# First block of a SwiGLU with block products: two k tiles by gate, then up columns, and token-sum chunks asked for by need

## What is computed

```python
x = x + jnp.concatenate([o_a, o_b], axis=-1) @ w_out[layer]
h = rms_norm(x, ffn_norm_w[layer])
gate, up = jnp.split(h @ w_gate_up[layer], 2, axis=-1)
x = x + (jax.nn.silu(gate) * up) @ w_down[layer]
```

## Time and profile before

| | |
|---|---|
| median of 3 runs | 1125.2 us (1123.52 to 1126.71) |
| the profiled execution | 1124.23 us |
| its span, first to last instruction | 1122.4 us |
| mean granted TensorE clock | 0.999 of full |
| busy PE, DVE, ACT, POOL | 1112.1, 900.1, 645.5, 53.0 us |
| instructions on PE | 5256 matmuls |
| transfers of w_gate_up and w_down | 176 and 88 of 512 KB |

### The profile page before, as it was taken

One profiled execution on the slowest core, in us unless ns is written; L12 is line 12 of the kernel. 1 busy time (PEld: TensorE's weight loads), 2 busy tenths in 40 slices (PEclk: granted clock), 3 DMA queues, 4 the chain that ended last, 5 costly groups with the idle time before them and its releaser, 6 DMA issues.

```text
span 1122.4 us, 15499 instructions
## 1 busy us (share of the span) xinstructions
PE 1112.1 (99%) x5256; PEld 936.2 (83%) x5256; DVE 900.1 (80%) x1222; ACT 645.5 (58%) x914; POOL 53.0 (5%) x138
## 2 busy tenths in 40 slices
PE   8999999999999999999999999999999999999998
PEld 7988888888888888888888888888888888888887
DVE  5578786587876667678988988988988889999887
ACT  7566776668654456454554554554554555655553
POOL 3000000000000000000000000000000020000000
PEclk9999999999999999999999999999999999999999
DMA  8666555545555455777787777777677786666665
GB/s 265 194 196 189 159 157 158 164 141 170 197 176 170 153 186 170 208 212 238 217 233 241 217 232 240 217 235 237 218 234 239 234 294 211 202 224 195 199 206 169
DMA packets 107558, 230.03 MB, mean 205 GB/s; under 512 B 8265, under 2 KB 19314, under 8 KB 107250
## 3 DMA queue, kind: packets, MB, share of 16 engines
q1 hardware_dynamic: 101346, 209.30, 60.3%
q0 software_dynamic: 5856, 19.93, 5.7%
q10 hardware_dynamic: 304, 0.14, 0.0%
HBM read 218.85 MB, written 10.49 MB: 204 GB/s over the span
## 4 chain that ended last, share of the span: by engine, by line
PE 93%; DVE 3%; DMA 2%; issue 1%; ACT 0%; SPq 0%; DVEq 0%; ACTq 0%
PE side L1928 22%; PE main L1700 22%; PE side L1930 11%; PE main L1703 11%; PE side L1898 4%; PE side L1899 4%; PE side L1900 4%; PE main L1899 3%; PE main L1900 3%; PE main L1898 3%; DMA raw<-in_w_down 1%; PE side L1824 1%; DMA raw<-in_w_in 1%; PE side L1723 1%; DVE w_lo L1542 1%
## 5 line engine op out<-in xcount | busy, mean ns | idle before, releaser
L985 ACT CAST w_hi<-raw 128x1024 fp32r<-128x1024 f32 x245 | 239.7, 984 | 162.2 <-PE side L1928 62.3
L1542 DVE TENSOR_TENSOR w_lo<-raw,w_hi 128x1024 fp32r<-128x1024 f32 x245 | 274.3, 1132 | 18.3 <-ACT w_hi L985 18.1
L1094 DVE TENSOR_TENSOR w_lo<-raw,w_hi 128x1024 fp32r<-128x1024 f32 (+3 forms) x156 | 178.6, 1154 | 108.1 <-ACT w_hi L765 105.8
L765 ACT CAST w_hi<-raw 128x1024 fp32r<-128x1024 f32 (+3 forms) x156 | 153.7, 994 | 142.3 <-PE main L1700 137.5
L1700 PE MATMUL main<-w_hi,hT_hi 128*128 128x512 f32 (+2 forms) x448 | 173.4, 388 | 1.7 <-DVE hT_lo L1115 1.2
L1703 PE MATMUL main<-w_hi,hT_lo 128*128 128x512 f32 (+2 forms) x448 | 169.1, 378 | 0.0
L1928 PE MATMUL side<-w_hi,hT_hi 128*128 128x512 f32 x400 | 155.6, 389 | 0.0
L1930 PE MATMUL side<-w_hi,hT_lo 128*128 128x512 f32 x400 | 155.6, 389 | 0.0
L1700 PE MATMUL main<-w_lo,hT_hi 128*128 128x512 f32 (+2 forms) x448 | 114.8, 378 | 0.0
L1928 PE MATMUL side<-w_lo,hT_hi 128*128 128x512 f32 x400 | 106.9, 389 | 0.0
L1700 PEld LDWEIGHTS main<-w_hi,hT_hi 128*128 128x128 f32 x448 | 84.8, 189 | 15.3 <-DVE hT_lo L1115 2.3
(11 more groups left out here) (283 smaller groups left out, 1853.0 us busy)
## 6 DMA issues: line engine op xcount, KB each, us to landing
raw<-in_w_gate_up SPq DMA_DIRECT2D x176, 512.0 KB, 4.8
raw<-in_w_down SPq DMA_DIRECT2D x88, 512.0 KB, 4.5
raw<-in_w_in SPq DMA_DIRECT2D x64, 512.0 KB, 3.8
raw<-in_w_out SPq DMA_DIRECT2D x32, 512.0 KB, 3.7
raw<-in_w_in SPq DMA_DIRECT2D x15, 384.0 KB, 5.1
squares<-hiddenT POOLq DMA_DIRECT2D x11, 512.0 KB, 5.1
hiddenT<-squares POOLq DMA_DIRECT2D x44, 128.0 KB, 5.4
raw<-in_w_ukv SPq DMA_DIRECT2D x8, 512.0 KB, 4.0
```

What stands on the lines that cost most here:

```text
L765: copy(w_hi[:, slot, 0:n], raw[:, slot, 0:n]).then_inc(s_hi, 1)
L985: copy(w_hi[:, n % RING, 0:cols], src).then_inc(s_hi, 1)
L1094: tt(w_lo[:, slot, 0:n], raw[:, slot, 0:n], w_hi[:, slot, 0:n].bitcast(F32), ALU.subtract)\
L1542: tt(w_lo[:, n % RING, 0:cols], src, w_hi[:, n % RING, 0:cols].bitcast(F32), ALU.subtract)\
```

## The change

Block 0 gets the layout of the others: the same 14 items, loads and conversions, with the banks swapped (`first_banks`: `main` as plain banks, `side` as m banks), the mix, the adds and the gated product of the loop. Its first two items, k tiles 4 and 5, run together: 12 matmuls on the gate columns of both, then 12 on the up columns, so that the second half of `main` is wanted later. `sum_ff_tokens` moves to G0-2, the copy of its hi part on ACT to G0-1, `split_ff_sums` to item 0 of block 0; the adds of `out2` 3 move ahead of item 3's conversion on DVE. PE's wait for all `side` uses moves from the head of the loop to block 0's first paired item. Chunk c of the token sums is asked for at W1 + 0, 7, 16, 28 or 40 granules.

```diff
-W1 = B1 + FF_W * (NFF - 1)
+W1 = G0 + FF_W * NFF
+FIRST_TOGETHER = 2
-FF_SUMS_AT = 6
+FF_SUMS_AT = G0 - 2
+SUMS_FROM = (0, 7, 16, 28, 40)
...
+        banks = ([[side[0], side[1]], [side[2], side[3]]], (main[PG][0], main[PG][1], main[PU][0], main[PU][1]))
+        first_banks = ([[main[PG][t], main[PU][t]] for t in range(NT)], (side[0], side[1], side[2], side[3]))
...
-                pool.wait_ge(s_used, W1 + 2 * c)
+                pool.wait_ge(s_used, W1 + SUMS_FROM[c])
...
+            for m in range(len(FF_ITEMS)):
+                convert_item(0, m)
+                for s in steps_at(G0 + m):
+                    step(s)
+                if m == FF_AT["corner"]:
+                    take_corner(0, first_banks[1][0])
+                if m == FF_AT["multiply"]:
+                    act.wait_ge(s_inv, len(RMS))
+                    silu(0)
...
+            for m in range(len(FF_ITEMS)):
+                steps = steps_at(G0 + m)
+                for s in steps:
+                    if s[0] == "out2":
+                        step(s)
+                convert_item(0, m)
+                for s in steps:
+                    if s[0] != "out2":
+                        step(s)
+                if m == 0:
+                    split_ff_sums()
+                if 0 <= m - FF_AT["mix"] < 4:
+                    mix(0, m - FF_AT["mix"], first_banks[1])
+                if m == FF_AT["add"]:
+                    add_gate_up(0, first_banks[0])
+                if m == FF_AT["multiply"]:
+                    multiply_gate(0)
...
+            def plain_begin_first(items):
+
+                for half in range(2):
+                    for x, (k, n) in enumerate(items):
+                        pe.wait_ge(s_tlo, SPLIT[("x2", k // 4, k % 4 // 2)] + 1)
+                        pe.wait_ge(s_lo, n + 1)
+                        for t in range(NT):
+                            if x == 0:
+                                pe.wait_ge(s_taken[(PG, PU)[half]], taken(FF - 2 + half) - NT + t + 1)
+                            m = three(first_banks[0][t][half][:, :], *ff_tokens(k, t),
+                                      *weights_of(n, NB * half, NB * (half + 1)), x == 0, False)
+                        if half:
+                            m.then_inc(s_used, 1)
...
+                if kind == "Q":
+                    if x == FF_FIRST:
+                        for engine in ("act", "dve"):
+                            pe.wait_ge(s_given[engine], max(n for u, n in GIVEN.items() if USES[u][1] == engine))
+                        pe.wait_ge(s_fflo, 1)
+                    paired(ff_tokens, ff_sums, FF_PAIR_TILES[which], which, n, 0, x == FF_FIRST, x == FF_LAST, first_banks)
+                    continue
```

More of the change, by code:

```diff
@@ L624, in load_gate_and_up @@
                         sp.dma_start(raw[:, slot, :].rearrange("p (h c) -> p h c", h=2), src).then_inc(s_raw[slot], 16)
-            for i in range(1, NFF):
+            for i in range(NFF):
                 load_gate_and_up(i)
@@ L967, in step @@
                     root(("r2a",), NT)
[L969 to L974, removed]
             def silu(i):
@@ L1024, in _ @@
                     step(s)
[L1026 to L1030, removed]
-                if j == KT // 2:
-                    act.wait_ge(s_inv, len(RMS))
-                    silu_first()
-                if j == FF_SUMS_AT + 2:
+                if g == FF_SUMS_AT + 1:
                     act.wait_ge(s_ffsum, 5)
@@ L1436, in step @@
                                   V_FFN + k + n) for n in range(2)])
-            def multiply_first():
-                dve.wait_ge(s_used, B1)
-                dve.wait_ge(s_taken[PG], taken(FF))
-                for t in range(NT):
-                    stt(out=hidden[:, t, :], in0=main[PU][t][:, :], scalar=r_ffn[:, t:t + 1], in1=gate[:, t, :],
-                        op0=ALU.mult, op1=ALU.mult).then_inc(s_hidden, 1)
             def multiply_gate(i):
@@ L1471, in add_gate_up @@
-            def add_gate_up(i):
-                dve.wait_ge(s_mixed, 4 * i)
+                    dve.wait_ge(s_mixed, 4 * i + 2)
+                    tt(gate[:, 1, :], gate[:, 1, :], m7[:, :], ALU.add).then_inc(s_mixed, 1)
+                else:
+                    dve.wait_ge(s_mixed, 4 * i + 3)
+                    tt(hidden[:, 1, :], gate[:, 1, :], m5[:, :], ALU.subtract).then_inc(s_mixed, 1)
+            def add_gate_up(i, plain):
+                dve.wait_ge(s_mixed, 4 * i + 4)
                 for n, (t, half) in enumerate(BANK_ORDER):
@@ L1917, in down_sums, with plain @@
                 return hi[:, p % 2, n, :], lo[:, p % 2, n, :]
[L1919 removed]
+            def plain(tokens, k, n, off, last=(), plain_bank=plain_bank):
                 pe.wait_ge(s_lo, n + 1 + off)
@@ L1955, in plain_end, with paired @@
                           True, True).then_inc(s_bank, 1)
-            def paired(tokens, sums, ks, p, n, off, first, last):
+            def paired(tokens, sums, ks, p, n, off, first, last, banks=banks):
                 k1, k2 = ks
+                plain_bank, (m1_bank, m5_bank, m6_bank, m7_bank) = banks
                 pe.wait_ge(s_lo, n + 1 + off)
```

151 lines of the change are left out of this document (70 added, 81 removed).

## The result

The changed kernel takes 1129.8 us (median of six runs, 1128.88 to 1131.84), the kernel before 1124.32 us (six runs, 1123.12 to 1126.71). The ratio is 1.0045, with a 95% interval of 1.0034 to 1.0055: slower, by a little more than the 0.36% forecast, and inside the range given. The profiled execution of the changed kernel is one of 1128.88 us with a span of 1126.8 us, 4.4 us longer than the span before.

A forecast was written before the change was run, and what follows sets the result against it. PE bounds the kernel, busy 1112.1 of 1122.4 us. Terms -1.36 - 0.40 - 1.0 + 0.5 + 4.65 give +2.4 us, +4.0 with the clock; on the median 1125.2 that is 1129.2 us, range 1126.3 to 1131.4.

The forecast's parts named there:

- 1: six matmuls: Block 0: two paired items replace four k tiles, six matmuls less on PE, a gain of 1.36 us.
- 2: step into block 1: Step from block 0 to block 1: PE waits for adds bank by bank, gaining the whole 0.40 us.
- Part 5: Ahead of item 5 in block 0: PE waits for `side` banks behind DVE's x2 split, a loss of 4.65 us.
- Part 4: Second half of `main`, block 0: PE waits for DVE's add of `out2` 3, a loss of 0.5 us.
- Part 6: Behind the `side` wait: clock at 1.2 GHz when PE goes on, 8 matmuls slow, a loss of 1.6 us.
- Part 3: Down projection: asking later for chunks 2 to 4 removes DVE's `first_two` stops, a gain of 1.0 us; later chunks cost nothing.
- the prediction's own sign: A stop of PE anywhere else in block 0 or at a later chunk would make the whole forecast wrong.
- The stop without the clock: Block 0: clock holds through the 4.5 us stop or returns within a matmul or two; +2.4 us, 1127.6; chance 0.25.
- The hidden stop: Block 0: x2 split of c = 3 is done early, PE never stands; -2.3 us, 1122.9; chance 0.08.
- the chunks change nothing: Down projection: weights come late as before, the 1.0 us stays; +5.0, 1130.2; chance 0.10.
- The lower clock for the whole paired item: Block 0: clock stays down through the first paired item; +6.6, 1131.8; chance 0.05.

The follow-up runs named there:

- e1: Changed kernel with block 0's split x2 of c = 3 ahead of item 5's conversion on ACT and DVE; 1122.16 us, ratio to before 0.9969.
- e5: Changed kernel, but in block 0 PE waits for each `side` bank where it first writes it; 1124.31 us, ratio to before 0.9990.
- e2: e1 with the token sums made one step earlier (G0 - 3 for G0 - 2); 1121.76 us, ratio to before 0.9965.
- e9: e1 with only block 0's first k tile run by gate, then up columns, not two; 1123.87 us, ratio to before 0.9988.
- e7: e6 with DVE making the fourth weight split three times over, so each of the ten stops is longer; 1196.47 us.
- e8: e2 with chunk 1 of the token sums asked for at granule 9 for 7; 1122.24 us, ratio to before 0.9977.
- e3: e1 with the old rule for asking for the chunks, every two granules; 1123.54 us, ratio to before 0.9987.
- e4: Kernel before with the later asks for the chunks as its only edit; 1123.76 us, ratio to before 0.9992.
- e10: Kernel before, unchanged, run once more for a second trace; 1124.34 us.
- e6: e1 with PE waiting in blocks 1 to 10, ahead of the first paired item, for its fourth weight set's split; 1156.51 us.

## Why the prediction was right

| part | forecast, us | profiled execution, us |
|---|---|---|
| 1: six matmuls | -1.36 | -1.36 |
| 2: step into block 1 | -0.40 | -0.40 |
| 3: chunks | -1.0 | -0.84 (traces: -1.1) |
| 4: second half of `main` | +0.5 | +0.58 |
| 5: wait for the `side` banks | +4.65 | +4.66 |
| 6: clock | +1.6 | +1.57 |
| a late start in a later block | - | +0.17 |
| sum | +4.0 | +4.4 |

**Part 5** was right in place, cause and size. It rested on reading a chain of hand-overs from another block's paired item, and adding the step that the new order puts behind it. e1 shows the place, e5 the banks. One sign was misjudged: the wait's releaser was to read DVE's hT_lo and reads "issue"; only where the wait was cut, in e5, did the view name it.

**Part 4** was right: 0.50 us and 0.08 for the new start, with the add of `out2` as releaser; e2 takes it away by the one edit that its cause suggests, and e9 shows what it would have been without the tiles running together.

**Part 6** was right in size, and its step was only half right. That the clock falls was read from one row, the end of the run, where it fell 1.9 us after PE's last matmul. This is the shortest such time of the thirteen traces; the others have 2.2 to 5.3 us. In the trace of e2 PE's last matmul begins at 1115.95 and lasts 0.28, and the clock is still at its higher level at 1121.40, 5.2 us later:

```profile
1119.80:1121.40 1.60, 0.00 (x0) 0.00 (x0) 0.00 (x0) 0.00 (x0) 0.00 (x0) 1.00 0.00 0
```

From that row the same argument would have said that the clock holds through 4.5 us. So the conclusion was right, but the row that gave it was a lucky one. The prediction also had the clock at the lower level when PE goes on, and it was at 1.00 until half a microsecond later. That eight matmuls run slowly was chosen between ends of 0 and 21; the count came true twice in this kernel, but e7 has 7 to 13, so the eight were partly luck, too. The Trainium skill, "TensorE: Matmul & The Clock Gate", Part 1, says that an idle array is throttled and gets its clock back after it has been kept busy; the second half, which no row of before showed, is seen in the trace of after, where the clock is back at 448.1, with PE at work all the way from 444.15.

**Part 3** was right in sign and about right in size, but its reason covers only part of it. The prediction had both stops of DVE at `first_two` go with chunks 2 to 4, and it costed these chunks at nothing where they are asked for now. The second stop did go from its place. The first stood in the trace of after with 1.95 us, and with 1.3 to 2.1 us in five others of the eight with the new asks; weights are late there as before. The hidden tile's own transfers and chunk 1 lie at that place, and e8, which moves chunk 1, could not tell them apart, so which of the two makes them late stays open. And the later chunks are not free: they brought DVE the stops listed above, and PE 0.28 us of late starts on the mean of the eight traces. In the trace of after the stop of 1.11 us behind chunk 2 did not reach PE. In four of the other seven traces PE does stop at a later chunk, which is the prediction's own sign that this term was too small.

**The median** rose by 5.5 us, the profiled execution by 4.65. The other executions of the changed kernel have spans of 1127.0 to 1129.9 us at a mean clock of 0.997 or 0.998, so some of them lose more to the clock than the traced ones; single executions of the kernel before are at 0.998 too, with spans near 1125 us. That the fall is longer in some executions, as it is from stop to stop in e7, would do it; so would a second fall of the kind that those executions of before seem to have, and one of the eight of e1 (0.998, 1.2 us longer than the traced one). No trace of such an execution was had, so this is argued, not shown. By the prediction's own account the forecast was made on the median of before, 1125.2; beside the changed kernel it was 1124.32. The base was 0.9 us too high and the change 1.5 us too small, so that the time came within 0.6 us is in part luck.

**The rivals.** The stop without the clock did not happen, but e5 is close to it: with the stop down to 1.51 us, the clock held. The hidden stop, 1122.9 us, was right about what it would be worth, and e1 is that case made on purpose: 1122.16 us. That the chunks change nothing is refuted by e3, e4 and e10. The lower clock for the whole paired item did not come.

## What to carry to other kernels

When a wait is moved to an earlier place, go through the lists of the engines that end it and look at what stands ahead of the last step that it needs; here one split stood behind a conversion that itself waited for PE, and moving that step turned a loss of 0.45% into a gain of 0.31%. A wait for all of a set of banks is best cut to the bank that is written next: that alone gave back 3.1 us of the stop and, because the rest was short, the clock as well. A transfer that is moved is to be costed where it goes: the chunks asked for later stopped DVE there. And a stop of a few microseconds on an otherwise full TensorE costs more than itself, here a third more (1.57 on 4.66).

## What the runs showed of the hardware

- The clock need not fall while PE stands. In this kernel it fell 0.5 us after PE had gone on from a stop of 4.4 us; in e6 1.1 to 1.5 us after, and only behind four of ten equal stops; in e7 within the stop, by 484.5 in the first and only after 535.0 in the second, where PE went on at 536.27. At the end of the thirteen traces it falls 1.9 to 5.3 us after PE's last matmul. So equal stops do not cost the same: 0 or 1.6 us behind 2.6 us, 1.55 to 2.8 us behind 5.2 us.
- At the lower level a matmul of 512 columns takes 0.427 us from start to start (444.69 to 447.68, seven of them), at the higher 0.227 us.
- A transfer beside the weights was not free though these were loaded three items ahead: 1.5 MB moved out of the first items of the down projection took 1.1 us of late starts off PE on the mean, and where the 1.5 MB went, 0.5 MB at a time, DVE stood for 0.3 to 2.3 us in 11 of 24 cases.
